# Two sparse-attention layers of a four-layer trunk: 15 projection tiles in place of 17, in another order, with other rotations

## The reference, cut to what matters

```python
def _dsa_mixer(h, pos, past_k, past_v, past_ki, w_in, w_out):
    Bn, T, _ = h.shape
    q, k, v, qi, ki, wi = jnp.split(h @ w_in, [A_O_Q, A_O_K, A_O_V, A_O_QI, A_O_KI], axis=-1)
    q = _rope(q.reshape(Bn, T, A_HEADS, A_HEAD_DIM), pos, A_ROT)
    k = _rope(k.reshape(Bn, T, A_KV_HEADS, A_HEAD_DIM), pos, A_ROT)
    v = v.reshape(Bn, T, A_KV_HEADS, A_HEAD_DIM)
    qi = _rope(qi.reshape(Bn, T, IDX_HEADS, IDX_DIM), pos, IDX_ROT)
    ki = _rope(ki, pos, IDX_ROT)
    ...
    def block(qb, qib, wib, pb):
        dots = jax.nn.relu(jnp.einsum('bthd,bsd->bths', qib.astype(F32), ki_all))
        score = jnp.einsum('bth,bths->bts', wib.astype(F32), dots) * iscale
        ...
        _, sel = lax.top_k(score, top)
        ...
        logits = jnp.einsum('btkgd,btskd->btkgs', qg, kg).astype(F32) * scale
        ...
        prob = jax.nn.softmax(logits, axis=-1).astype(vg.dtype)
        o = jnp.einsum('btkgs,btskd->btkgd', prob, vg)
    ...
    return o @ w_out, k, v, ki
```

## Time and profile before

| | |
|---|---|
| median of 3 runs | 1723.79 us (1719.29 to 1725.69) |
| the profiled execution: its own time | 1720.39 us |
| its span in the profile | 1718.6 us |
| mean granted clock of TensorE | 0.986 of full speed |
| PE busy | 95% |
| DVE, ACT, POOL busy | 66%, 50%, 42% |

### The profile page before, as it was taken

One profiled execution on the slowest core, in us unless ns is written; L12 is line 12 of the kernel. 1 busy time (PEld: TensorE's weight loads), 2 busy tenths in 40 slices (PEclk: granted clock), 3 DMA queues, 4 the chain that ended last, 5 costly groups with the idle time before them and its releaser, 6 DMA issues.

```text
span 1718.6 us, 37190 instructions
## 1 busy us (share of the span) xinstructions
PE 1637.5 (95%) x14005; PEld 1555.8 (91%) x14005; DVE 1134.6 (66%) x2021; ACT 859.5 (50%) x1618; POOL 725.3 (42%) x786
## 2 busy tenths in 40 slices
...
GB/s 217 86 50 137 157 147 154 135 151 101 99 99 32 4 10 77 108 160 151 150 119 151 161 107 32 118 151 152 153 130 148 158 83 74 147 147 146 124 146 107
DMA packets 344399, 205.22 MB, mean 119 GB/s; under 512 B 22376, under 2 KB 340120, under 8 KB 344160
## 3 DMA queue, kind: packets, MB, share of 16 engines
...
q10 hardware_dynamic: 384, 0.88, 0.2%
...
## 4 chain that ended last, share of the span: by engine, by line
PE 81%; DVE 7%; issue 3%; ACT 3%; POOL 3%; SPq 1%; DMA 1%; DVEq 0%; ACTq 0%; POOLq 0%
PE bank L910 23%; PE bank L911 22%; PE bank L912 22%; PE bank L1322 5%; ACT hi L1596 1%; PE bank L922 1%; DVE lo L2126 1%; PE bank L1233 1%; DVE SW L2325 1%; SPq L549 1%; PE bank L972 1%; PE bank L1346 1%; DVE top L2322 1%; POOL qcos L676 1%; PE bank L1330 1%
## 5 line engine op out<-in xcount | busy, mean ns | idle before, releaser
L910 PE MATMUL bank<-XH,hi 128*128 128x320 f32 x1960 | 618.3, 315 | 12.5 <-ACT qraw L2047 2.8
L2126 DVE TENSOR_TENSOR lo<-raw,hi 128x2048 fp32r<-128x2048 f32 (+1 forms) x195 | 418.4, 2146 | 293.4 <-ACT hi L1596 293.4
L912 PE MATMUL bank<-XH,lo 128*128 128x320 f32 x1960 | 609.1, 311 | 0.0
L911 PE MATMUL bank<-XL,hi 128*128 128x320 f32 x1960 | 609.0, 311 | 0.0
L1596 ACT ACTIVATE hi<-raw 128x2048 fp32r<-128x2048 f32 (+1 forms) x203 | 357.6, 1762 | 77.0 <-PE bank L912 61.7
L910 PEld LDWEIGHTS bank<-XH,hi 128*128 128x128 f32 x1960 | 370.9, 189 | 26.3 <-issue 13.0
L911 PEld LDWEIGHTS bank<-XL,hi 128*128 128x128 f32 x1960 | 371.2, 189 | 1.5 <-issue 0.2
L912 PEld LDWEIGHTS bank<-XH,lo 128*128 128x128 f32 x1960 | 370.8, 189 | 0.0
L706 POOL TENSOR_TENSOR upad<-upad,rstd 128x128 f32<-128x128 f32 (+1 forms) x176 | 168.8, 979 | 198.9 <-ACT upad L1696 198.9
L910 PE MATMUL bank<-GH,hi 128*128 128x322 f32 x704 | 220.0, 312 | 1.8 <-DVE lo L2126 1.8
L911 PE MATMUL bank<-GL,hi 128*128 128x322 f32 x704 | 218.7, 311 | 0.0
...
## 6 DMA issues: line engine op xcount, KB each, us to landing
...
```

The source lines that it names most:

```text
L910: pe.matmul(out, a, xh(k), start=(start and k == 0), stop=False)
L911: pe.matmul(out, a, xl(k), start=False, stop=False)
L912: last = pe.matmul(out, b, xh(k), start=False, stop=(stop and k == kt - 1))
L2126: dve.tensor_tensor(lo[n % 2][:, 0:w_], raw[n % 2][:, 0:w_], hi[n % 2][:, 0:w_].bitcast(F32), ALU.subtract).then_inc(w_lo, 1)
```

## The change

Only the two sparse layers change, and with them the layout in which four of the inputs are handed over and three outputs are returned.

- The columns of `w_in` are handed over in another order: index queries, index key, index weights with 56 columns of zeros, keys, values, queries. Query heads are paired so that the two heads of a pair belong to different key/value heads; `KT` then holds both key heads once, on 64 partitions each. The rows of `w_out` are reordered to suit.
- There are 15 tiles: 0 to 3 index queries, 4 index key and index weights together, 5 both key heads, 6 values, 7 to 14 queries. Each slab is one load.
- Index queries are rotated with the plain tables, without 1/rms. The index weights are multiplied by 1/rms twice instead. (The relu of a positive multiple is the multiple of the relu.)
- Cached keys and index keys are handed over transposed and go straight into `KT` and `KIT`. New keys, values and index keys are stored as they lie. So only the index weights (after tile 5) and the values (after tile 9) are turned on TensorE.
- Tile 7 and tile 8 are made in halves between the score dots.

TensorE, layer 0, from the end of the ninth tile to the first score dots, before. `ck`, `ci` are the cached keys; `con` is the identity matrix.

The diff, cut to its core:

```diff
+def sparse_columns(w):
+
+    k, v, qi, ki, wi = (w[:, :, a:b] for a, b in ((1024, 1152), (1152, 1280), (1280, 1792), (1792, 1856), (1856, 1864)))
+    return np.concatenate([qi, ki, wi, np.zeros_like(w[:, :, 0:56]), k, v, w[:, :, A_PAIRS]], axis=2)
...
             begin((layer, "mix"))
-            k, v, ki, wi = 1024, 1152, 1792, 1856
-            slabs.append(Slab("kk", 0, 8, 264, [(0, cols(w, k, 64)), (64, cols(w, k, 64)), (128, cols(w, k + 64, 64)),
-                                                (192, cols(w, k + 64, 64)), (256, cols(w, wi, 8))], 3))
-            slabs.append(Slab("kiv", 0, 8, 256, [(0, cols(w, ki, 64)), (64, cols(w, ki, 64)), (128, cols(w, v, 128))], 2))
-            for j in range(2):
-                slabs.append(Slab("qi", j, 8, 256, [(0, cols(w, 1280 + 256 * j, 256))], 2))
-            for j in range(4):
-                slabs.append(Slab("q", j, 8, 256, [(0, cols(w, 256 * j, 256))], 2))
+            for j in range(8):
+                width = 128 if j == 3 else 256
+                slabs.append(Slab("in", j, 8, width, [(0, cols(w, 256 * j - 128 * (j > 3), width))], width // 128))
...
@@ -816,34 +813,39 @@
                 if mixer == 0:
                     if inst:
                         pool.wait_ge(x_done, 8 * xs_of[norm_of[layer, "mix"]] + 8)
+                    pool.dma_start(KT[:, 0:PAST], i_["cache_a_k"][inst]).then_inc(cache_in, 16)
                     for dup in range(2):
-                        for g in range(2):
-                            pool.dma_start(ck[:, g, dup, :], i_["cache_a_k"][inst, 0, :, g, :]).then_inc(cache_in, 16)
-                        pool.dma_start(ci[:, dup, :], i_["cache_a_idx"][inst, 0]).then_inc(cache_in, 16)
+                        pool.dma_start(KIT[64 * dup:64 * dup + 64, 0:PAST], i_["cache_a_idx"][inst]).then_inc(cache_in, 16)
                     pool.dma_start(Vc[:, :], i_["cache_a_v"][inst, 0].rearrange("p g d -> p (g d)")).then_inc(cache_in, 16)
+                    new = slice(PAST, KEYS)
+                    pool.wait_ge(con_rest, 16)
+                    for j in range(2):
+                        rope(R0[layer] + j, E0[layer] + j + 1, C("cos_a"), C("sin_a"), QIT[:, j, :])
                     pool.wait_ge(rstd_done, norm_of[layer, "mix"] + 1)
-                    pool.wait_ge(con_rest, 16)
                     pool.tensor_tensor(cosr[:, :], C("cos_a"), rstd[:, :], ALU.mult)
                     pool.tensor_tensor(sinr[:, :], C("sin_a"), rstd[:, :], ALU.mult).then_inc(cosr_done, 1)
+                    for j in range(2, 4):
+                        rope(R0[layer] + j, E0[layer] + j + 1, C("cos_a"), C("sin_a"), QIT[:, j, :])
                     pool.wait_ge(cosr_done, inst + 1)
-                    new = slice(PAST, KEYS)
-                    dsts = [KT[:, 0, new], KT[:, 1, new], KIT[:, new], QIT[:, 0, :], QIT[:, 1, :], QIT[:, 2, :], QIT[:, 3, :]]
-                    for r_, t_ in enumerate(A_ROPE[:9 - 2]):
-                        rope(R0[layer] + r_, E0[layer] + t_ + 1, cosr[:, :], sinr[:, :], dsts[r_])
-                    for z, (c, n_) in enumerate(TILES):
-                        pool.wait_ge(rows_out, ROWS_BEFORE[layer] + z + 1)
-                        if z == 0:
-                            dst = [o_[q][inst, 0] for q in ("a_k_sample", "a_v_sample", "a_idx_sample")]
-                        else:
-                            dst = [o_[q][inst, 0, 128 * (z - 1):128 * z] for q in ("a_k_prompt", "a_v_prompt", "a_idx_prompt")]
-                        store(dst[0].rearrange("p g d -> p (g d)"), Ko[0:n_, z, :])
-                        store(dst[1].rearrange("p g d -> p (g d)"), Vt[0:n_, z, :])
-                        store(dst[2], KIo[0:n_, z, :])
+                    r4 = R0[layer] + 4
+                    rope_cos(r4, E0[layer] + 5, cosr[0:64, :], 64)
+                    c_, s_ = qcos[0:64, r4 % 2, :], qsin[0:64, r4 % 2, :]
+                    pool.wait_ge(swap_done, r4 + 1)
+                    chain(pool.tensor_tensor(s_, s_, sinr[0:64, :], ALU.mult))
+                    pool.wait_ge(cos_done, r4 + 1)
+                    chain(pool.tensor_tensor(KIT[64:128, new], c_, s_, ALU.add))
+                    pool.tensor_tensor(KIT[0:64, new], c_, s_, ALU.add).then_inc(rope_done, 1)
+                    rope(R0[layer] + 5, E0[layer] + 6, cosr[:, :], sinr[:, :], KT[:, new])
+                    pool.wait_ge(rope_done, R0[layer] + 6)
+                    pool.wait_ge(v_scaled, inst + 1)
+                    store(o_["a_k"][inst], KT[:, new])
+                    store(o_["a_v"][inst], VTf[:, :])
+                    store(o_["a_idx"][inst], KIT[0:64, new])
...
+                def values_turn():
+                    pe.wait_ge(v_scaled, inst + 1)
+                    pe.wait_ge(relu_done, 8 * inst + 6)
+                    for z, (c, n_) in enumerate(TILES):
+                        last = turn(psum[2][0:n_, 128 * z:128 * z + 128], VTf[:, c:c + n_])
+                    last.then_inc(v_turned, 1)
+
+                def tile_part(t, first, end):
+                    product(psum[q_bank(t)][:, 0:T], s0 + slab_of[t], col_of[t], lambda k: XH[:, k, :], lambda k: XL[:, k, :],
+                            first=first, end=end)
+
+                for t in range(0 if layer else 2, 7):
                     project(t)
-
+                    if t == 5:
+                        weights_turn()
+
+                pe.wait_ge(rope_done, Rb + 5)
+                pe.wait_ge(tile_evac, E + 6)
                 pe.wait_ge(cache_in, 16 * CACHE_LOADS[layer])
-                for g in range(2):
-                    turn(psum[3][:, 128 * g:128 * g + 128], ck[:, g, :, :].rearrange("p u d -> p (u d)"))
-                turn(psum[3][:, 256:384], ci[:, :, :].rearrange("p u d -> p (u d)")).then_inc(turned, 1)
-
-                pe.wait_ge(rope_done, Rb + 3)
-                pe.wait_ge(rows_scaled, inst + 1)
-                for z, (c, n_) in enumerate(TILES):
-                    b = psum[(6, 7, 4)[z]]
-                    for g in range(2):
-                        turn(b[0:n_, 64 * g:64 * g + 64], KT[0:64, g, PAST + c:PAST + c + n_])
-                    turn(b[0:n_, 128:256], VTf[:, c:c + n_])
-                    turn(b[0:n_, 256:320], KIT[0:64, PAST + c:PAST + c + n_])
-                    turn(b[0:n_, 320:448], WIf[:, c:c + n_]).then_inc(rows_turned, 1)
-
-                pe.wait_ge(rope_done, Rb + 7)
-                pe.wait_ge(turned_in, inst + 1)
-                pe.wait_ge(rows_out, ROWS_BEFORE[layer] + 3)
+
                 def dots(h2):
                     if h2 >= 2:
                         pe.wait_ge(relu_done, 8 * inst + 2 * h2 - 2)
...
                 dots(0)
+                ready(s0 + slab_of[7])
+                tile_part(7, 0, 4)
+                pe.wait_ge(wi_out, inst + 1)
                 dots(1)
-                ready(s0 + slab_of[9])
-                pe.wait_ge(tile_evac, E + 8)
-                tile_part(9, 0, 4)
+                tile_part(7, 4, None)
                 dots(2)
-                tile_part(9, 4, None)
+                pe.wait_ge(tile_evac, E + 7)
+                tile_part(8, 0, 4)
                 dots(3)
+                tile_part(8, 4, None)
                 def pair_qk(p):
-                    pe.wait_ge(rope_done, Rb + 8 + p)
+                    pe.wait_ge(rope_done, Rb + 7 + p)
                     if p == 0:
+                        pe.wait_ge(rope_done, Rb + 6)
                         pe.wait_ge(relu_done, 8 * inst + 8)
-                    qk(Q + p, lambda e: QD[64 * e:64 * e + 64, p, :], lambda e: KT[64 * e:64 * e + 64, p // 4, :], 64)
-
-                def tile_15(low):
-                    n = s0 + slab_of[15]
...
                             pe.matmul(out, wh[:, k, c], XL[:, k, :], start=False, stop=False)
 
-                for t in range(10, 15):
+                for t in range(9, 13):
                     project(t)
+                    if t == 9:
+                        values_turn()
                 pair_qk(0)
-                tile_15(False)
+                tile_13(False)
                 pair_qk(1)
-                tile_15(True)
-                pe.wait_ge(tile_evac, E + 15)
...
-                firsts = {0: 0, 3: 1, 5: 2, 7: 3, 11: 5, 13: 6}
+                firsts = {0: 0, 2: 1, 4: 2, 6: 3, 9: 5, 11: 6}
...
-                    if t == (0 if layer else 1):
+                    if t == 1:
                         root(norm_of[layer, "mix"])
...
-                for t in range(9):
+                    act.activation(dst, psum[q_bank(t)][:, 0:T], ACT.Copy, scale=-1.0 if t >= 7 else 1.0).then_inc(tile_evac, 1)
+
+                for t in range(6):
                     evac(t)
+                act.wait_ge(wi_turned, inst + 1)
                 for z, (c, n_) in enumerate(TILES):
-                    act.wait_ge(rows_turned, ROWS_BEFORE[layer] + z + 1)
-                    b = psum[(6, 7, 4)[z]]
-                    act.copy(Ko[0:n_, z, :], b[0:n_, 0:128])
```

(31 more changed lines are left out.)

110 lines of the change are left out of this document (58 added, 52 removed).

## The result

The changed kernel takes 1711.37 us (median of 4 runs, 1710.17 to 1713.07), the kernel before 1722.34 us beside it (4 runs); the ratio is 0.9937, with an interval of [0.992, 0.9954]. So it is faster by 0.5 to 0.8%. The profiled execution took 1710.17 us with a span of 1708.4, against 1720.39 and 1718.6: 10.2 us gained, where 20.6 were forecast.

The account below looks back on a forecast made before the run. PE, busy 95% of the span, was taken to bound the kernel until the last dots, VectorE after them. Terms of -11.9 (layer 0), -8.3 (layer 3) and -0.4 gave -20.6 us: 1701.5 us, range 1693 to 1711.

Parts of the forecast that it names:

- start-up *gain: Start of the kernel: another 2 us gained there, allowed for only in the range's lower end of 1693 us.
- larger pieces move faster: Slab loads: pieces of 1 KB load at about 400 GB/s, where pieces of 256 bytes and less move at about 200.
- Ahead of the mean square, -1.48: Layer 0: slab 1 lands earlier, so PE's wait of 1.48 us ahead of the mean square goes; bounds 0 and -1.48.
- Two tiles, -7.04, transposes, -2.3, GpSimd's wait, -0.2: Layer 0 before the dots: two tiles fewer, -7.04 us; 18 transposes become 3, -2.3; GpSimd's wait 1.5 for 1.67, -0.2.
- Clock at the dots, -2.7: Layer 0, score dots: the clock stays up instead of falling, -2.7 us; bounds 0 and -3.1.
- 1.5 tiles, +1.8: Layer 0, between the dots: tile 7 and half of tile 8 where one tile lay, +1.8 us.
- Layer 3, -8.3: Layer 3 until the last dots: fewer tiles and transposes, no 0.80 us wait, half a tile more; -8.3 us.
- The constant of VectorE: Last dots to second `pair_qk`, both layers: VectorE's summing and picking keep this stretch at 23.2 us.
- After the last dots, -0.4: Both layers: PE's idle time before the second `pair_qk` grows to about 2.0 us at no cost; pair loop -0.2 each.
- The slower rival: Second `pair_qk`: the clock falls and stays down, up to 30 us a layer, 1760 us; chance 0.03.
- the GpSimd rival: Layer 0: GpSimd's rotations end late, dots wait 4 us, clock falls, gain only 12 us, 1708 to 1712; chance 0.17.
- PE alone: Whole kernel: PE's own sum decides, scoring and picking do not; 24.3 us gained, 1696 to 1699.5 us; chance 0.15.

Follow-up runs that it names:

- e1: Changed kernel, with SyncE issuing the rest of the constants and what follows only once the vectors have landed; 1706.96 us, ratio 0.9917 to the kernel before.
- e2: Changed kernel, with slab 0 loaded by four loads of 64 columns instead of one; 1707.86 us, ratio 0.9918 to the kernel before.
- e5: Changed kernel, with the vectors' load issued by SyncE, third in its queue ahead of slab 0, not by GpSimd; 1704.87 us, ratio 0.9894 to the kernel before.
- e4: Changed kernel, with one of the eight key-picking rounds left out, so fewer keys are picked; 1705.80 us, ratio 0.9904 to the kernel before.
- e3: Changed kernel, with 18 unread filling matmuls ahead of the second `pair_qk` in both layers; 1709.68 us, ratio 0.9924 to the kernel before.
- e6: Changed kernel, with index queries rotated by the scaled tables again and index weights scaled once, keeping 15 tiles; 1721.52 us, ratio 0.9996 to the kernel before.
- e7: Changed kernel, with 14 unread filling matmuls ahead of the first dots of layer 0; 1711.64 us, ratio 0.9930 to the kernel before.
- e8: Changed kernel with the edits of e5, e3 and e7 together; 1702.53 us, ratio 0.9886 to the kernel before.

## Why the prediction was wrong, step by step

The direction was right and the size was not. The step that failed is one that the sum did not have: it let TensorE start when it did before. Only a start-up *gain* was allowed for, in the lower end of the range. Fewer, larger loads were read as faster loads. What they did as well was to take SyncE from 9.8 us of issuing to 0.43, and so put 1616 KB of constants and slab 1 ahead of the vectors: +4.87 us in the trace, some 3 to 7 us in e1, e2 and e5. The last 1.5 of the 4.87 us are not shown to come from them (e1).

The reading that larger pieces move faster was half right. The rates of the changed kernel and of e2, 0 to 12 us in 40 equal slices:

```profile
GB/s 0 0 0 0 0 10 96 28 124 213 342 407 380 410 400 423 410 437 427 318 188 201 208 164 174 160 188 314 345 355 338 355 348 450 541 215 526 308 617 330
...
GB/s 1 0 0 0 0 17 76 45 137 247 284 366 387 396 413 410 437 410 410 389 178 200 157 160 136 125 191 217 216 218 237 326 254 358 341 461 404 248 282 283
```

The low rate from 6.3 to 8.1 us, which the prediction put down to short pieces, is there with pieces of 1 KB too: 160 to 208 GB/s in the changed kernel. From 8.1 to 9.0 us they then move at 314 to 355 GB/s, where e2's pieces of 256 bytes move at 216 to 218.

- *Ahead of the mean square, -1.48:* right; ScalarE begins to split slab 1 at 19.77 instead of 22.91 us, and the wait is gone, in e5 also with the early start. A further 0.63 us went with it.
- *Two tiles, -7.04, transposes, -2.3, GpSimd's wait, -0.2 (together -9.54):* measured -8.60. GpSimd's wait is 2.18 us, inside the 0.6 to 2.6 given but not the 1.5 taken. Unforeseen was 0.71 us for `WIf`: VectorE scales it twice only after the swap of tile 4, and that swap waits 2.20 us for GpSimd to free its buffer. One `lo` subtraction hit GpSimd's last operation, which the prediction had priced.
- *Clock at the dots, -2.7, and 1.5 tiles, +1.8 (together -0.9):* measured +0.91. "I take it that it stays up" was wrong: after 2.18 us of waiting it was at a mean of 0.63 for 4.3 us, so only 1.5 of 3.1 us came back. The tiles between the dots cost 13.01 - 10.57 = 2.4 us in layer 3, not 1.8.
- *Layer 3, -8.3:* -8.35, and no wait ahead of the dots. That it fits so closely is partly luck: the way to the first dots shortened by 10.78 us where the terms give 10.14, and the tiles between the dots cost 2.4 instead of 1.8.
- *The constant of VectorE:* 23.38 and 23.37 us where 23.22 and 23.21 were. e4 shows that it is one.
- *After the last dots, -0.4:* the idle time came out as 2.69 instead of 2.0 us, "it costs nothing by itself". It came with a fall of the clock that cost 1.7 us in each layer of this execution. The slower rival named exactly this place, yet wanted a clock that stays down. Its counter-argument, that 1.83 us of idling had left the clock at 1.00, does not hold in general either: behind the same wait it fell in e3, e4, e6, e7 and e8. A fall of 4.4 us that recovers stood only in the GpSimd rival, once, as +2 us; the forecast's sum had no term for it.
- *The rivals:* the time fell where "GpSimd takes the tiles' place" had it (1708 to 1712), but mostly for another reason. Its 4 us of waiting and its lost 1.48 us did not occur, its falls of the clock did. e6 shows the rival in full. "PE alone" falls with the two equal stretches of 23.4 us.

The errors are 4.87 (start), -0.63 and 0.94 (to the dots), 1.81 (dots), 0.3 (constant) and 3.1 (after `pair_qk`, 2.75 lost where 0.4 was to be gained): 10.4, the difference between 20.6 and 10.2. Nearly half of it is the start. It was in reach: the rows of 9.76 and 11.47 us stood in the trace, and only the issue time of each load behind them had to be worked out anew.
